# Hand-over between stages: four blocks by token halves, weights four deep, residual adds on VectorE

## Chip, cores and metric

One core of a Trainium2 chip runs the whole kernel. The metric is the device time in microseconds (us) of one execution. Outputs are compared with a float32 reference.

## What is computed

512 tokens and 16 meta tokens of width 1024 pass two layers (differential attention, then a short convolution, each followed by a squared-ReLU MLP of width 4096) and then a third block of pooling and a linear recurrence. All of it hangs on this pattern, four times over:

```python
hres = hres + _rmsnorm(m, norm_g[i, 1])
h = _rmsnorm(hres, norm_g[i, 2])
hres = hres + _rmsnorm(_sqrelu_mlp(h, w_up[i], w_down[i]), norm_g[i, 3])
```

and at the end `x = x + y @ w_out[l]`, `rmsnorm(x, final_gain)`. A stage's output `m` is normed and added to the residual `hres`; its norm is the next stage's input.

## The kernel before

Activations lie transposed: 128 channels on the partitions, KT = 8 rows of channels, and 528, 514 or 512 tokens along the free axis (ALL, NEED, OUT). The token halves part at SPLIT = 272. Each of the 225 weight **blocks** (128 output channels by 1024 inputs) is loaded by SyncE into `raw` (four slots), rounded by ScalarE to `whi` (`split`, L502 and in loops L513), and GpSimd subtracts to get the rest `wlo` (`low`, L442). TensorE makes 8 x 3 products a block (whi x hi, whi x lo, wlo x hi, L1329): in two token pieces where there are over 512 tokens, and in one where there are 512. `whi` and `wlo` have two slots, so the split of block b + 2 waits until block b is done. Blocks alternate between two accumulators in PSUM, `G[0]` and `G[1]` (two banks each); `begin` waits until the block two before was copied out.

Every engine runs its own list in order. Four times a stage ends in an RMS norm and the next starts: index i = 0 (attention output, block b0 = 24 onwards, to the first MLP), 1 (to the convolution input), 2 (convolution output to the second MLP), 3 (to the third block's input projection, blocks 192 to 216, where a chain of feature work for four head pairs runs on ScalarE and VectorE under the blocks). At such a **hand-over**:

- TensorE (`last_blocks`) does blocks 6 and 7 of the old stage by token halves, first halves first, then the second halves with the norm's sum (`post_stat`, L1313 and L1317) for the first half of the tokens between them. `first_blocks` then does the new stage's blocks 0 and 1 by halves; block 0 goes row by row behind VectorE, with a product that sums the next norm's squares (`stat_tile`, L1302) before each row.
- VectorE (`last_tiles`) copies the tiles out (L855, L858), adds their squares (L849), takes the reciprocal of the root (L832), scales a row by gain and rstd into `t1` (L897), and makes the low part of the input (`low_x`, L838).
- GpSimd (`residual`, L450) adds `t1` to `hres`; ScalarE (`prenorm`) rounds the row to `xh` (L537) and squares it (L541).

In an MLP's first product each block is copied out with ReLU and rstd (L934), squared twice on ScalarE, and VectorE makes the low part (L925). After block 216, GpSimd makes the four pooled groups (L475 to L487); TensorE's four products of them stand among the steps of the recurrence.

## Time and profile before

| | us |
|---|---|
| median of 3 runs (lowest, highest) | 1746.52 (1742.81, 1751.23) |
| the profiled execution, its time | 1749.39 |
| its span in the trace | 1747.6 |
| TensorE busy (94% of the span) | 1648.2 |
| VectorE, ScalarE, GpSimd busy | 773.7, 621.3, 623.2 |

The mean granted clock of TensorE is 0.974 of full speed. A matmul counts as busy until its result is out, so in a stretch where each waits for the one before, TensorE reads as busy and yet does less than it can: the number of matmuls in a stretch says more than its busy time.

### The profile page before, as it was taken

What the parts mean: (1) busy time and instruction counts of PE and PEld (TensorE: products, weight loads), DVE (VectorE), ACT (ScalarE), POOL (GpSimd) and SP (SyncE); (2) the same over time, 40 slices, a digit from 0 to 9 for tenths busy, and PEclk for the clock granted to TensorE, in tenths of its full rate; (3) what the DMA queues carried; (4) which work ended last, traced back from release to release, by engine and by line L of the source; (5) the groups of instructions that cost most, each with busy time, mean ns of one, the idle gap of its engine ahead of it and who ended that gap; (6) DMA issues with size and microseconds to landing.
All of it is one profiled execution on the core that took longest, in us unless ns stands there. A gap on an engine that the chain in (4) does not pass through costs nothing.

```text
span 1747.6 us, 31109 instructions
## 1 busy us (share of the span) xinstructions
PE 1648.2 (94%) x12448; PEld 1441.7 (82%) x12448; DVE 773.7 (44%) x1260; ACT 621.3 (36%) x1127; POOL 623.2 (36%) x315
## 2 busy tenths in 40 slices
PE   7999998899999999899998999999998999899895
PEld 6888876889999999799977788888886777777664
DVE  3334442554232221654427441414138995455426
ACT  5556663343222222422224432313135434232312
POOL 2222221444444344444435444444435444500021
PEclk9999998999999999999999999999999999899888
DMA  5112110222332322123221333333321222000001
GB/s 194 51 49 61 50 49 25 73 73 86 97 90 92 97 87 96 61 73 96 86 90 42 97 97 96 96 90 93 95 85 61 73 88 93 15 3 2 2 25 48
DMA packets 35400, 125.64 MB, mean 72 GB/s; under 512 B 3920, under 2 KB 4048, under 8 KB 35280
## 3 DMA queue, kind: packets, MB, share of 16 engines
q1 hardware_dynamic: 35280, 123.90, 22.6%
q8 instruction: 93, 1.52, 0.4%
q14 instruction: 27, 0.22, 0.0%
HBM read 121.79 MB, written 2.10 MB: 71 GB/s over the span
## 4 chain that ended last, share of the span: by engine, by line
PE 80%; DVE 11%; POOL 3%; issue 3%; ACT 2%; DMA 0%; DVEq 0%; SPq 0%; POOLq 0%; ACTq 0%
PE G L1329 63%; PE G L1571 4%; PE PV L1571 3%; PE PV L1444 2%; DVE t L897 2%; PE ST L1571 2%; DVE rstd L832 1%; POOL wlo L442 1%; PE PO L1571 1%; DVE xl L838 1%; PE G L1420 1%; PE ST L1302 1%; POOL t L475 1%; PE PO L1433 1%; DVE t L1088 1%
## 5 line engine op out<-in xcount | busy, mean ns | idle before, releaser
L442 POOL TENSOR_TENSOR wlo<-raw,whi 128x1024 fp32r<-128x1024 f32 x225 | 547.5, 2434 | 1065.2 <-ACT whi L502 704.2
L1329 PE MATMUL G<-xh,whi 128*128 128x256 f32 (+3 forms) x1552 | 387.2, 313 | 4.7 <-POOL wlo L442 2.7
L1329 PE MATMUL G<-xl,whi 128*128 128x256 f32 (+3 forms) x1552 | 368.5, 301 | 0.0
L1329 PE MATMUL G<-xh,wlo 128*128 128x256 f32 (+3 forms) x1552 | 366.7, 300 | 0.0
L1329 PE MATMUL G<-ah,whi 128*128 128x258 f32 (+2 forms) x992 | 269.6, 319 | 10.7 <-POOL wlo L442 6.2
L1329 PEld LDWEIGHTS G<-xh,whi 128*128 128x128 f32 x1552 | 251.3, 189 | 29.9 <-issue 11.3
L513 ACT ACTIVATE whi<-raw 128x1024 fp32r<-128x1024 f32 x112 | 118.8, 1060 | 429.5 <-PE G L1329 429.5
L1329 PE MATMUL G<-al,whi 128*128 128x258 f32 (+2 forms) x992 | 267.2, 317 | 0.0
L1329 PE MATMUL G<-ah,wlo 128*128 128x258 f32 (+2 forms) x992 | 266.9, 316 | 0.0
L1329 PEld LDWEIGHTS G<-xl,whi 128*128 128x128 f32 x1552 | 250.9, 189 | 12.4
L1329 PEld LDWEIGHTS G<-xh,wlo 128*128 128x128 f32 x1552 | 251.8, 189 | 10.2
L502 ACT ACTIVATE whi<-raw 128x1024 fp32r<-128x1024 f32 x113 | 119.5, 1058 | 288.7 <-PE G L1329 254.4
L1329 PEld LDWEIGHTS G<-ah,whi 128*128 128x128 f32 x992 | 169.4, 191 | 25.6 <-POOL wlo L442 7.2
L1329 PEld LDWEIGHTS G<-al,whi 128*128 128x128 f32 x992 | 168.8, 191 | 12.7
L1329 PEld LDWEIGHTS G<-ah,wlo 128*128 128x128 f32 x992 | 168.6, 191 | 12.7
L925 DVE TENSOR_TENSOR al<-act,ah 128x512 f32 (+2 forms) x64 | 115.7, 1807 | 98.3 <-ACT act L582 98.3
L858 DVE TENSOR_TENSOR m<-G,m 128x514 f32 (+5 forms) x52 | 33.9, 651 | 209.3 <-PE G L1329 209.3
L934 DVE SCALAR_TENSOR_TENSOR t<-G,rstd 128x514 f32<-128x514 f32 (+1 forms) x64 | 44.3, 693 | 105.8 <-PE G L1329 105.5
L1329 PE MATMUL G<-x2h,whi 128*128 128x512 f32 (+1 forms) x216 | 87.5, 405 | 0.9 <-POOL wlo L442 0.9
L1302 PE MATMUL ST<-sq,con 128*128 128x256 f32 (+2 forms) x160 | 56.4, 446 | 28.8 <-DVE xl L838 21.6
L1329 PE MATMUL G<-x2l,whi 128*128 128x512 f32 (+1 forms) x216 | 82.0, 380 | 0.0
L1329 PE MATMUL G<-x2h,wlo 128*128 128x512 f32 (+1 forms) x216 | 81.6, 378 | 0.0
(275 smaller groups left out, 2023.8 us busy)
## 6 DMA issues: line engine op xcount, KB each, us to landing
raw<-weights_dram SPq DMA_DIRECT2D x225, 512.0 KB, 3.5
hres<-xT_dram SPq DMA_DIRECT2D x8, 264.0 KB, 6.0
out_dram<-hres SPq DMA_DIRECT2D x8, 256.0 KB, 2.1
con<-consts_dram SPq DMA_DIRECT2D x1, 512.0 KB, 9.2
mat<-mats_dram SPq DMA_DIRECT2D x1, 512.0 KB, 10.0
con<-consts_dram SPq DMA_DIRECT2D x1, 392.0 KB, 5.5
vec<-vecs_dram SPq DMA_DIRECT2D x1, 203.0 KB, 2.6
```

What stands on the lines that cost most here:

```text
L442: nc.gpsimd.tensor_tensor(wlo[:, s % 2], raw[:, s], whi[:, s % 2].bitcast(F32), ALU.subtract)\
L475: nc.gpsimd.tensor_tensor(dst[:, PAD:], src[:, PAD:], src[:, PAD - sh:PAD + SEQ - sh], ALU.add)\
L502: nc.scalar.activation(whi[:, s % 2], raw[:, s], ACT.Copy).then_inc(hi_ready, 1)
L513: nc.scalar.activation(whi[:, s2 % 2], raw[:, s2], ACT.Copy).then_inc(hi_ready, 1)
L858: nc.vector.tensor_tensor(mt, acc_of[:, pos], mt, ALU.add).then_inc(count, 1)
L897: nc.vector.scalar_tensor_tensor(t1[:, k % 2, o], m[:, k, o], gain(*norm, k), rstd[:, s % 2, tokens(cols, half)], ALU.mult, ALU.mult)\
L925: nc.vector.tensor_tensor(tile(al[f % 2], j, slice(0, w)), act2[:, s4 % 2, 0:w], tile(ah[f % 2], j, slice(0, w)).bitcast(F32), ALU.subtract)\
L934: nc.vector.scalar_tensor_tensor(t1[:, s4 % 2, 0:w], G[s4 % 2][:, pos], 0.0, rstd[:, s % 2, c0], ALU.max, ALU.mult).then_inc(tile_out, 1)
L1302: last = nc.tensor.matmul(ST[:, p0:p1], ones, sq[:, k % 2, t0 - cols[0]:t1_ - cols[0]], start=k == 0, stop=k == KT - 1, skip_group_check=True)
L1329: last_of[0] = nc.tensor.matmul(to[:, p0:p1], wt[:, w, ws], xt[:, k, t0 - off:t1_ - off], start=k == 0 and q == 0, stop=k == KT - 1 and q ...
L1444: last = nc.tensor.matmul(PV[0:rows, 0:P], aT[0:nk, t % 2, j, 0:rows], vtok[0:nk, h % 2, j, :], start=j == 0, stop=j == i)
L1571: return nc.tensor.matmul(out_, lhsT, rhs, start=start, stop=stop)
```

## The change

`whi` and `wlo` get four slots and `raw` two. The old stage's blocks 4 to 7 go by token halves (four first halves, then four second halves), and so do the new stage's blocks 0 to 3: blocks 0 and 1 side by side row by row, then blocks 2 and 3. Blocks done by halves have banks of their own (`held`). VectorE takes over the residual add, and the low parts of the new stage's first four weight blocks (`low_w`). The squares for the next norm go into four half-wide slots of `t1`, and TensorE sums them two rows late. In the third block's input projection blocks 4 and 5 move up to steps 2 and 3. In the attention stage the weight split runs three blocks ahead instead of two. Some buffers of the third block now share memory with others.

VectorE's queue at the first hand-over (`m` is the stage's output, `t` is t1, `acc` the sum of squares), before: from the first reciprocal on.

```order
L832 RECIPROCAL rstd<-rms 128x258 [waits rms_ready]
L897 SCALAR_TENSOR_TENSOR t<-m,vec,rstd 128x258 [waits rstd_ready]
L855 COPY m<-G 128x256 [waits block_done]
L897 SCALAR_TENSOR_TENSOR t<-m,vec,rstd 128x258
L849 TENSOR_TENSOR acc<-acc,sq 128x256 [waits psq_added,psq_ready]
L855 COPY m<-G 128x256 [waits block_done]
L897 SCALAR_TENSOR_TENSOR t<-m,vec,rstd 128x258 [waits h_ready]
L838 SCALAR_TENSOR_TENSOR xl<-hres,vec,xh 128x258 [waits x_hi]
```

The same place in the changed kernel, up to the second row:

```order
L869 RECIPROCAL rstd<-rms 128x258 [waits rms_ready]
L893 COPY m<-G 128x256 [waits block_done]
L928 SCALAR_TENSOR_TENSOR m<-m,vec,rstd 128x258 [waits rstd_ready]
L928 SCALAR_TENSOR_TENSOR m<-m,vec,rstd 128x258
L935 TENSOR_TENSOR hres<-hres,m 128x258 [waits t1_ready]
L928 SCALAR_TENSOR_TENSOR m<-m,vec,rstd 128x258
L935 TENSOR_TENSOR hres<-hres,m 128x258 [waits t1_ready]
L876 SCALAR_TENSOR_TENSOR xl<-hres,vec,xh 128x258 [waits x_hi]
L893 COPY m<-G 128x256 [waits block_done]
L887 TENSOR_TENSOR acc<-acc,sq 128x256 [waits psq_added,psq_ready]
L908 TENSOR_TENSOR wlo<-raw,whi 128x1024 [waits hi_ready]
L928 SCALAR_TENSOR_TENSOR m<-m,vec,rstd 128x258
```

The add of a row and the wide subtraction of a weight block (L908) now stand in VectorE's own queue, where a wait for GpSimd (`h_ready`) stood.

TensorE's queue where the new stage begins (`sq` and `t1` hold squares, `acc` their sum), before:

```order
L1313 MATMUL ST<-acc,con 128x256 [waits psq_added,rms_ready]
L1317 MATMUL ST<-sq,con 128x256 [waits psq_ready]
L1302 MATMUL ST<-sq,con 128x258 [waits rms_ready,x_ready,sq_ready,tile_out,lo_ready]
L1329 MATMUL G0<-xh,whi 128x258
L1329 MATMUL G0<-xl,whi 128x258
L1329 MATMUL G0<-xh,wlo 128x258
L1302 MATMUL ST<-sq,con 128x258 [waits sq_ready,x_ready]
```

and in the changed kernel, from the first row of the new stage:

```order
L1416 MATMUL G0<-xh,whi 128x258 [waits tile_out,lo_ready,x_ready]
L1416 MATMUL G0<-xl,whi 128x258
L1416 MATMUL G0<-xh,wlo 128x258
L1416 MATMUL G0<-xh,whi 128x258
L1416 MATMUL G0<-xl,whi 128x258
L1416 MATMUL G0<-xh,wlo 128x258
L1416 MATMUL G0<-xh,whi 128x258 [waits x_ready]
```

A row now carries six matmuls instead of three, the sum of squares stands two rows behind, and the second half's post_stat has moved behind row 4. The diff, cut to its core:

```diff
-POST_SQ, POST_ADD = KT + 2, KT
+HELD = 4
+POST_SQ, POST_ADD = KT + HELD, KT + HELD - 2
+def half_square(j, half):
+    return j + 1 + (HELD if half else 0)
+def half_added(j, half):
+    return j + 1 + (HELD - 1 if half else 0)
+def square_slot(k, half):
+    q = k + KT * half
+    return q % 2, TOK // 2 * (q // 2 % 2)
+def held(cols, j, half):
+    w = cols[1] - cols[0]
+    first = SPLIT - cols[0]
+    if half is None:
+        return [(j, 0, 0, w)] if w <= BANK else [(j, 0, 0, first), ((6, 7, 4, 5)[j], 0, first, w)]
+    if half == 0:
+        return [(j, 0, 0, first)]
+    return [(j, first, first, w)] if w <= BANK else [((6, 7, 4, 5)[j], 0, first, w)]
...
-        raw = sb("raw", [P, 4, D])
-        whi = sb("whi", [P, 2, D], F32R)
-        wlo = sb("wlo", [P, 2, D], F32R)
+        raw = sb("raw", [P, 2, D])
+        whi = sb("whi", [P, 4, D], F32R)
+        wlo = sb("wlo", [P, 4, D], F32R)
...
-            act2 = sb("act2", [P, 2, NW], F32, mlp)
             cb = sb("cb", [P, 3, NW], F32, mlp)
+            act2 = cb[:, 0:2]
...
-                if isinstance(b, int) and b < 4:
+                if isinstance(b, int) and b < 2:
                     return
-                sp.wait_ge(lo_ready, b - 3)
+                sp.wait_ge(lo_ready, b - 1)
                 src = weights[b] if isinstance(b, int) else weights[bass.ds(b, 1)].rearrange("b p n -> p (b n)")
-                sp.dma_start(raw[:, s], src).then_inc(w_loaded[s], 16)
+                sp.dma_start(raw[:, s % 2], src).then_inc(w_loaded[s % 2], 16)
             blocks(sp, 0, NBLK, load)
...
-                if not isinstance(b, int) or b >= 2:
-                    pool.wait_ge(block_done, b - 1)
-                nc.gpsimd.tensor_tensor(wlo[:, s % 2], raw[:, s], whi[:, s % 2].bitcast(F32), ALU.subtract)\
+                if not isinstance(b, int) or b >= 4:
+                    pool.wait_ge(block_done, b - 3)
+                nc.gpsimd.tensor_tensor(wlo[:, s], raw[:, s % 2], whi[:, s].bitcast(F32), ALU.subtract)\
...
-            def residual(i, half, cols):
-                for k in range(KT):
-                    n = 2 * KT * i + KT * half + k + 1
-                    pool.wait_ge(t1_ready, n)
-                    c = tokens(cols, half)
-                    nc.gpsimd.tensor_tensor(hres[:, k, c], hres[:, k, c], t1[:, k % 2, tokens(cols, half, cols[0])], ALU.add)\
-                        .then_inc(h_ready, 1)
             done = 0
-            for i, (b, cols) in enumerate(((B_MLP[0], NEED), (B_CI, NEED), (B_MLP[1], OUT), (B_IN2, OUT))):
-                blocks(pool, done, b + 1 - done, low)
-                residual(i, 0, cols)
-                low(b + 1, 1, (b + 1) % 4)
-                residual(i, 1, cols)
-                done = b + 2
-            blocks(pool, done, B_O2 + 2 - done, low)
+            for b in (B_MLP[0], B_CI, B_MLP[1], B_IN2):
+                blocks(pool, done, b - done, low)
+                done = b + HELD
+            blocks(pool, done, B_O2 + 3 - done, low)
...
-                        split(b + 2, (s + 2) % 4)
+                        split(b + HELD, s)
...
+                def input_row(k, half):
+                    if k < KT:
+                        c = tokens(cols, half)
+                        act.wait_ge(h_ready, 2 * KT * i + KT * half + k + 1)
+                        hi = x2h[:, k, tokens(cols, half, META)] if layer == 2 else xh[:, k, c]
+                        nc.scalar.activation(hi, hres[:, k, c], ACT.Copy, scale=gain(layer, n, k)).then_inc(x_hi, 1)
+                    if k >= 2:
+                        input_square(k - 2, half)
+                def input_square(k, half):
+                    c = tokens(cols, half)
+                    if k + KT * half >= 4:
+                        act.wait_ge(sq_used, sq_base(s) + KT * half + k - 3)
+                    r, o = square_slot(k, half)
+                    nc.scalar.activation(t1[:, r, o:o + c.stop - c.start], hres[:, k, c], ACT.Square).then_inc(sq_ready, 1)
+                for j in range(HELD, KT):
+                    half_square_of(j, 0)
+                stat_root(s - 1, cols, 0)
+                split(new, 0)
+                half_square_of(4, 1)
+                input_row(0, 0)
+                input_row(1, 0)
+                half_square_of(5, 1)
+                split(new + 1, 1)
+                input_row(2, 0)
+                input_row(3, 0)
+                half_square_of(6, 1)
+                split(new + 2, 2)
+                input_row(4, 0)
+                input_row(5, 0)
+                half_square_of(7, 1)
+                split(new + 3, 3)
+                input_row(6, 0)
+                stat_root(s - 1, cols, 1)
+                for k in range(7, KT + 2):
+                    input_row(k, 0)
+                stat_root(s, cols, 0)
+                for k in range(KT + 2):
+                    input_row(k, 1)
+                stat_root(s, cols, 1)
...
-                    split(s + 2, (s + 2) % 4)
+                    split(s + 3, (s + 3) % 4)
...
+            def low_w(b):
+                dve.wait_ge(hi_ready, b + 1)
+                nc.vector.tensor_tensor(wlo[:, b % 4], raw[:, b % 2], whi[:, b % 4].bitcast(F32), ALU.subtract)\
+                    .then_inc(lo_ready, 1)
...
+                def scaled(k, half):
+                    o = tokens(cols, half, cols[0])
+                    nc.vector.scalar_tensor_tensor(m[:, k, o], m[:, k, o], gain(*norm, k), rstd[:, s % 2, tokens(cols, half)],
+                                                   ALU.mult, ALU.mult).then_inc(t1_ready, 1)
+                def residual(k, half):
+                    c = tokens(cols, half)
+                    dve.wait_ge(t1_ready, 2 * KT * i + KT * half + k + 1)
+                    nc.vector.tensor_tensor(hres[:, k, c], hres[:, k, c], m[:, k, tokens(cols, half, cols[0])], ALU.add)\
+                        .then_inc(h_ready, 1)
+                def input_rows(ks, half):
+                    for k in ks:
+                        if k + 1 < KT:
+                            scaled(k + 1, half)
+                        residual(k, half)
+                        if k >= 1:
+                            low_x(i + 1, *pre, k - 1, cols, half)
...
-                half_tile(KT - 2, 0)
-                add_square(i, KT - 3, cols)
-                half_tile(KT - 1, 0)
-                add_square(i, KT - 2, cols, 0)
-                for half in range(2):
-                    stat_recip(s, cols, half)
-                    dve.wait_ge(rstd_ready, stat_count(s, half))
-                    o = tokens(cols, half, cols[0])
-                    for k in range(KT + 2):
-                        if k < KT:
-                            if k >= 2:
-                                dve.wait_ge(h_ready, 2 * KT * i + KT * half + k - 1)
-                            nc.vector.scalar_tensor_tensor(t1[:, k % 2, o], m[:, k, o], gain(*norm, k),
-                                                           rstd[:, s % 2, tokens(cols, half)], ALU.mult, ALU.mult)\
-                                .then_inc(t1_ready, 1)
-                        if k == 5 and half == 1:
-                            stat_recip(s + 1, cols, 0)
-                        if k >= 2:
-                            low_x(i + 1, *pre, k - 2, cols, half)
-                        elif k == 0 and half == 0:
-                            half_tile(KT - 2, 1)
-                        elif k == 1 and half == 0:
-                            add_square(i, KT - 2, cols, 1)
-                            half_tile(KT - 1, 1)
+                for j in range(HELD, KT):
+                    half_tile(j, 0)
+                    add_square(i, j - 1, cols, None if j == HELD else 0)
+                stat_recip(s, cols, 0)
+                half_tile(4, 1)
+                dve.wait_ge(rstd_ready, stat_count(s, 0))
+                scaled(0, 0)
+                input_rows((0, 1), 0)
+                half_tile(5, 1)
+                add_square(i, 4, cols, 1)
+                low_w(new)
+                input_rows((2, 3), 0)
+                half_tile(6, 1)
+                add_square(i, 5, cols, 1)
+                low_w(new + 1)
+                input_rows((4, 5), 0)
+                half_tile(7, 1)
+                add_square(i, 6, cols, 1)
+                low_w(new + 2)
+                input_rows((6, 7), 0)
+                stat_recip(s, cols, 1)
+                low_x(i + 1, *pre, KT - 1, cols, 0)
+                low_w(new + 3)
+                stat_recip(s + 1, cols, 0)
+                dve.wait_ge(rstd_ready, stat_count(s, 1))
+                scaled(0, 1)
+                input_rows(range(KT), 1)
+                low_x(i + 1, *pre, KT - 1, cols, 1)
...
-                post_stat(s - 1, cols, 1)
+                off = META if hi is x2h else 0
+                def rows(j, ks, half):
+                    (g, p0, o0, o1), = held(cols, j, half)
+                    some(bank(g), j, ks, hi, lo, off, [(cols[0] + o0, cols[0] + o1, p0, p0 + o1 - o0)])
+                def start(j):
+                    pe.wait_ge(lo_ready, b0 + j + 1)
+                    pe.wait_ge(tile_out, b0 + j - 3)
                 for half in range(2):
-                    for j in range(2):
+                    if half == 0:
+                        start(0)
+                        start(1)
+                    for k in range(KT):
+                        pe.wait_ge(x_ready, x_base(i + 1) + KT * half + k + 1)
+                        if k >= 2:
+                            stat_tile(s, k - 2, cols, half)
+                        for j in range(2):
+                            rows(j, [k], half)
+                            if half and k == KT - 1:
+                                last_of[0].then_inc(block_done, 1)
+                        if k == 4 and half == 0:
+                            post_stat(s - 1, cols, 1)
+                    stat_tile(s, KT - 2, cols, half)
+                    stat_tile(s, KT - 1, cols, half)
+                    for j in range(2, HELD):
                         if half == 0:
-                            begin(b0 + j)
-                        for k in range(KT):
-                            if j == 0:
-                                pe.wait_ge(x_ready, x_base(i + 1) + KT * half + k + 1)
-                                stat_tile(s, k, cols, half)
-                            some(G[(b0 + j) % 2], (b0 + j) % 2, [k], hi, lo, 0, block_part(cols, half))
+                            start(j)
+                        else:
+                            pe.wait_ge(rms_ready, stat_count(s, j - 2))
+                        rows(j, range(KT), half)
                         if half:
                             last_of[0].then_inc(block_done, 1)
             def last_blocks(i, b0, hi, lo, cols):
-                operands = hi, lo, cols[0]
-                for j in (KT - 2, KT - 1):
-                    begin(b0 + j)
-                    some(G[j % 2], j % 2, range(KT), *operands, part(cols, 0))
+                def rows(j, ks, half):
+                    t = tokens(cols, half)
+                    some(bank(j - HELD), j % 4, ks, hi, lo, cols[0], [(t.start, t.stop, 0, t.stop - t.start)])
+                for j in range(HELD, KT):
+                    pe.wait_ge(lo_ready, b0 + j + 1)
+                    pe.wait_ge(tile_out, b0 + (HELD - 1 if j < HELD + 2 else HELD))
+                    rows(j, range(KT), 0)
                     last_of[0].then_inc(half_done, 1)
-                some(G[0], 0, range(KT // 2), *operands, part(cols, 1))
-                post_stat(2 * i + 1, cols, 0)
-                some(G[0], 0, range(KT // 2, KT), *operands, part(cols, 1))
-                last_of[0].then_inc(block_done, 1)
-                some(G[1], 1, range(KT), *operands, part(cols, 1))
-                last_of[0].then_inc(block_done, 1)
+                for j in range(HELD, KT):
+                    pe.wait_ge(half_out, HELD * i + j - HELD + 1)
+                    if j == HELD:
+                        rows(j, range(3), 1)
+                        post_stat(2 * i + 1, cols, 0)
+                    rows(j, range(3 if j == HELD else 0, KT), 1)
+                    last_of[0].then_inc(block_done, 1)
...
-                elif j >= 2:
-                    product(B_IN2 + j, 1, x_ready, 0, x2h, x2l, OUT, 0)
+                elif j in (2, 3) or j >= 6:
+                    ahead = j + 2 if j < 4 else j
+                    product(B_IN2 + ahead, 1, x_ready, 0, x2h, x2l, OUT, 0)
...
```

## Rows read from the trace of the kernel before

**Rows 1.** The page: busy time of each engine.
```profile
PE 1648.2 (94%) x12448; PEld 1441.7 (82%) x12448; DVE 773.7 (44%) x1260; ACT 621.3 (36%) x1127; POOL 623.2 (36%) x315
```

**Rows 2.** Windows: PE, PEld, DVE, ACT, POOL busy, granted clock, DMA.
```profile
327.00:363.50 36.50, 29.36 (x182) 25.64 (x180) 30.05 (x42) 19.84 (x44) 19.72 (x19) 0.95 0.09 30
1341.20:1484.10 142.90, 140.84 (x584) 107.38 (x584) 117.50 (x116) 62.24 (x73) 60.41 (x23) 1.00 0.28 86
```

**Rows 3.** The chain that ended last: start, us, what.
```profile
294.96 24.80 PE G L1329 x192
320.99 2.39 POOL wlo L442
329.41 1.78 DVE rstd L832
363.45 344.44 PE G L1329 x2880
...
717.53 1.78 DVE rstd L832
...
752.83 126.12 PE G L1329 x1056
...
962.11 334.11 PE G L1329 x1440
```

**Rows 4.** Timeline of DVE, first hand-over.
```profile
326.94 0.42 DVE L849 TENSOR_TENSOR acc<-acc,sq 128x258 f32<-128x258 f32 x1
331.95 2.28 DVE L897 SCALAR_TENSOR_TENSOR t<-m,vec,rstd 128x258 f32<-128x258 f32 x1
...
336.72 0.48 DVE L897 SCALAR_TENSOR_TENSOR t<-m,vec,rstd 128x258 f32<-128x258 f32 x1
337.12 0.47 DVE L838 SCALAR_TENSOR_TENSOR xl<-hres,vec,xh 128x258 fp32r<-128x258 f32 x1
337.51 0.86 DVE L897 SCALAR_TENSOR_TENSOR t<-m,vec,rstd 128x258 f32<-128x258 f32 x1
338.30 0.47 DVE L838 SCALAR_TENSOR_TENSOR xl<-hres,vec,xh 128x258 fp32r<-128x258 f32 x1
...
361.74 0.69 DVE L934 SCALAR_TENSOR_TENSOR t<-G,rstd 128x514 f32<-128x514 f32 x1
363.82 0.69 DVE L925 TENSOR_TENSOR al<-act,ah 128x514 fp32r<-128x514 f32 x1 [1.39 <-ACT act L582]
364.43 0.69 DVE L934 SCALAR_TENSOR_TENSOR t<-G,rstd 128x514 f32<-128x514 f32 x1
```

**Rows 5.** Timeline of POOL: in the first hand-over, and behind block 216.
```profile
331.54 2.39 POOL L442 TENSOR_TENSOR wlo<-raw,whi 128x1024 fp32r<-128x1024 f32 x1 [8.18 <-ACT whi L502]
...
1487.64 1.03 POOL L475 TENSOR_TENSOR t<-zu 128x512 f32<-128x512 f32 x1
```

**Rows 6.** Timeline of PE; idle time before in brackets.
```profile
294.96 0.51 PE L1329 MATMUL G<-ah,whi 128*128 128x258 f32 x2 [2.92 <-POOL wlo L442]
...
326.39 0.28 PE L1329 MATMUL G<-ah,whi 128*128 128x256 f32 x1
...
341.17 0.60 PE L1302 MATMUL ST<-sq,con 128*128 128x258 f32 x2
...
341.97 0.60 PE L1302 MATMUL ST<-sq,con 128*128 128x258 f32 x2
...
1512.32 2.07 PE L1571 MATMUL PV<-Gp,mat 128*128 128x512 f32 x2 [4.28 <-POOL Gp L487]
```

**Rows 7.** Windows behind two long waits, columns as above.
```profile
297.00:299.00 2.00, 2.00 (x11) 2.00 (x11) 0.00 (x0) 0.00 (x0) 0.44 (x1) 0.50 0.80 238
1512.30:1516.00 3.70, 3.68 (x34) 2.17 (x36) 1.18 (x2) 0.00 (x0) 0.00 (x0) 0.50 0.00 0
```

**Rows 8.** The page: weight splits and transfers (median us to landing).
```profile
L502 ACT ACTIVATE whi<-raw 128x1024 fp32r<-128x1024 f32 x113 | 119.5, 1058 | 288.7 <-PE G L1329 254.4
...
raw<-weights_dram SPq DMA_DIRECT2D x225, 512.0 KB, 3.5
```

181 lines of the change are left out of this document (86 added, 95 removed).

## Prediction

> **What bounds the kernel now.** I read the page first: TensorE is busy 94% of the span [rows 1]. Then the chain: two stages run as one piece of TensorE work, 2880 matmuls in 344.4 us and 1056 in 126.1 [rows 3]; that is 0.1195 us for 257 columns, 2.87 us a half block and 5.74 a block, and 344.44 is 60 blocks with nothing to gain. With 512 columns a block takes 24 x 334.11/1440 = 5.57. What is left lies at the seams. In the first hand-over, 327.0 to 363.5, TensorE starts 182 matmuls in 36.5 us [rows 2], where its pace allows 305: some 15 us go although it reads as busy. The chain there runs over VectorE's reciprocals and its rows. VectorE's timeline shows why a row takes 1.18 us: scale, then low part, 0.40 and 0.39 apart when alone, but 0.79 when GpSimd's add runs beside them (337.51 to 338.30), and 2.28 for one beside the subtraction of a weight block that began at 331.54 [rows 4, 5]. TensorE has three products and a sum for each row, 0.80 us (341.17 to 341.97) [rows 6].
>
> **The hand-over before.** I count from the end of block 3 of the old stage to the start of block 4 of the new one. Blocks 4 and 5 take 11.5, first half of 6 2.9, then the wait for block 7's wlo (split after block 5, landing at 320.99 + 2.39, 1.2 us late [rows 3]), first half of 7 2.9: 18.5. There the second halves start, at 326.39 [rows 6]; the reciprocal follows 3.0 later, at 329.41, and the new stage's block 2 at 363.45, that is 37.05 behind 326.39. At the next one I put the second halves 3.0 ahead of 717.53 and get 752.83 - 714.5 = 38.3; the two others give the same 38.3. With blocks 2 and 3 (11.5) the first costs 67.0 and the others 68.3 (67.6 with 512 columns).
>
> **The hand-over after.** No wait for wlo, since four slots let it run ahead: four first halves, 11.5. Call the start of the second halves 0.
> - TensorE: three rows, post_stat at 1.1 to 1.8 (now after three rows and not four), the rest of block 4 to 3.6, blocks 5 to 7 to 12.2.
> - VectorE, with these steps between starts: scale 0.40, low part 0.39, 258-column add or copy 0.35 (0.42 long, 326.94), reciprocal 1.68 [rows 4]. `low_w` is not in the trace: a 514-column subtraction takes 0.69, a 258-column one 0.42, so 1024 columns take about 1.23. The bounds are 1.15 and GpSimd's 2.39. Reciprocal 2.7 to 4.4; rows 0 and 1, then a copy, an add, low_w: first one done 8.9, second 13.0, third 17.1.
> - TensorE waits at block 1's start for the second low_w, 12.2 to 13.05. Rows of six products: 0.80 + 3 x 0.12 = 1.15 (0.72 for the first two, which carry no sum). Row 4 ends 17.95, post_stat 18.65, row 6 20.95. The second reciprocal runs 19.5 to 21.2, the last low part lands 21.6, row 7 ends 22.8, the sums 23.5, the first halves of blocks 2 and 3 29.25.
> - Meanwhile VectorE: low_w, reciprocal of the new norm 24.4 to 26.2, then eight rows of 0.40 + 0.35 + 0.40 = 1.15. It ends at 35.4, and TensorE, which starts these rows at 29.25, is never held: rows end 38.3, second halves of blocks 2 and 3 44.0. Last reciprocal 39.2 to 41.0.
> - Block 4 needs blocks 0 to 2 copied out. In an MLP a block costs VectorE the 2.69 from 361.74 to 364.43, of which it waits 1.39 for the squares [rows 4]: 41.0 + 2 x 2.69 + 0.7 = 47.1, and 0.7 more for one low part held up by GpSimd's 2.39 instruction: third block out at 47.8. In the convolution input there is no such wait: out by 43.1, TensorE goes on at 44.0.
>
> Of the moved work, sixteen adds cost VectorE 5.6 us a hand-over and four low_w 4.6; the sixteen 0.39 us stalls and the 1.8 at 331.95 that go with GpSimd's silence pay 8. GpSimd's queue holds nothing else there. The new transfers for blocks 2 and 3 start only when low_w 0 and 1 free a raw slot, and land 3.5 later [rows 8], at 12.4 and 16.5; ScalarE waits for them in order, but it was busy only 19.8 of 36.5 us [rows 2].
>
> **The sum.**
> - First hand-over: 67.0 - (11.5 + 47.8) = 7.7, less 2.0: a wait of 3.8 us on TensorE is followed by a lower clock. Behind the 2.92 us wait at 294.96 [rows 6] the granted clock reads 0.50, the 1.2 GHz level [rows 7], and 192 matmuls take 24.80 instead of 22.95 [rows 3]: 1.85. Gain 5.7.
> - Second: 68.3 - 55.5 = 12.8, less 0.6 for block 5, which finds VectorE in the convolution: 12.
> - Third: 67.6 - 59.3 - 2.0 = 6.3.
> - Fourth: here the feature chain on VectorE counts too. From 1341.2 to 1484.1 TensorE does 23 blocks of 5.57 (128.1) and the feature products in 142.9, with VectorE busy 117.5 [rows 2]. The upper bound is TensorE alone: 68.3 - 55.5 = 12.8, and some 5 of waits in that stage: 18. The lower bound is VectorE's start on the new blocks: before at 361.74 - 326.39 + 1.25 + 18.5 = 55.1 behind block 3 [rows 4, 6], now at 52.5: 2.6. Between them: before, VectorE's steps 2 to 5 each waited for a block 5.57 apart and then ran late; now blocks 0 to 3 lie ready, and it has caught up when the first pair's sums arrive behind block 5. Walking its queue so, I get the pair's chain 9 us earlier, and take 9.
> - Start of the attention output: its third block waited 2.92 for wlo [rows 6], since two slots were full. Now blocks 2 and 3 are ready; 0.2 remains for the copy-out. 2.7 and the 1.85 of clock: 4.5.
> - Pooling: GpSimd starts it at 1487.64 because the last weight block before it is split behind block 216. Now the last is split behind block 215, 5.57 earlier. TensorE waits 4.28 for the fourth group at 1512.32 [rows 5, 6], and then runs at 0.50 at least to 1516 [rows 7]. The wait goes whole; of the clock I take 3, between the 1.85 found above and half of the stretch if it lasts to about 1522. 7.3.
> - Weights two deep in raw at the start, and one split more ahead of row 6: -0.5.
>
> 5.7 + 12 + 6.3 + 9 + 4.5 + 7.3 - 0.5 = 44.3. The profiled execution took 1749.4, 2.9 above the median; 1749.4 - 44.3 = 1705.1, against the median 1702.
>
> **Two rules of the Trainium skill.** "VectorE: DVE Perf Modes", section on the TRN2 errata, says each SBUF instruction pays a fixed cost, so many small tiles lose against few large ones; this speaks against halves. The trace agrees (0.42 twice against 0.69: 0.15 a split); the sum above has it in its durations, and by the page's (N+151)/0.96 cycles low_w would be 1.22, an estimate that moves nothing. "TensorE: Matmul & The Clock Gate", section on HAM oscillation, says that idle gaps put TensorE back to half rate; the trace agrees (0.50 behind 2.92 idle). Without it the sum would be 44.3 - 4.85 + 4 = 43.5.
>
> **Rivals.**
> - *VectorE becomes the bound of the hand-over* (0.18). It carries every add now. If the steps don't fall to 0.40 (sixteen at 0.79), each hand-over gives back 6.2: 25 us, 1727. For it: the deep mix of semaphores, and VectorE already 30 of 36.5 us busy [rows 2]; against it: 336.72 to 337.12 shows 0.40 with GpSimd quiet.
> - *TensorE nearly dense* (0.14): the copy-out waits vanish behind slack (2 x 5.8) and the fourth hand-over gives 12 instead of 9: 1702 - 15 = 1687.
> - *Slower by the raw ring* (0.04): a raw slot is reused after split 1.06, low 2.39 and transfer 3.5, 7.0 us [rows 5, 8], against two blocks, 11.5. From a transfer of 8.0 us on, every 0.1 costs 0.05 a block, 9 us over some 190 blocks; at 8.5 us it eats the 44, at 8.6 it gives 1711 + 44 = 1755. For it: transfers of the start take longer when many run at once; against it: the median of 3.5 over 225 [rows 8].
> - *The change does nothing that counts* (0.05): what TensorE saves in rows comes back as waits for copy-out and features, at every hand-over: 1742 to 1750.
>
> The forecast itself has 0.59, with its own range 1692 to 1714. The range goes to 1685 and 1728, which takes in the first two rivals. What a measurement can tell is about 0.5%, 9 us. Faster 0.91, same 0.05, slower 0.04.
>
> **What would show it.** Right: four hand-overs of TensorE shortened by about 8, 12, 8 and 9; VectorE rows of 1.15 with no GpSimd instruction beside; no wait for wlo at 295, 321, 709; the fourth pooled group without a wait; a copy-out wait near 3.8 in both MLPs and none in the convolution. Wrong: rows at 1.5 or more; waits of ScalarE for raw in the long stages; the feature chain ending where it did.

## The result, and the profile after

The changed kernel takes 1730.9 us (median of 20 runs, 1715.7 to 1747.0), the kernel before 1746.8 beside it: ratio 0.989, 95% interval 0.9874 to 0.9907. (The ratio is that of the fast runs, which leaves out six of the 20 of the changed kernel.) It is faster, by 16 us where 44 were forecast, and it lies above the range. The profiled execution took 1724.9 us, its span is 1723.0. The forecast's own range was 1692 to 1714, the full one 1685 to 1728.

The page of the changed kernel, busy time of each engine, answers to [rows 1]:
```profile
PE 1644.7 (95%) x12640; PEld 1451.2 (84%) x12640; DVE 792.9 (46%) x1364; ACT 621.7 (36%) x1135; POOL 530.2 (31%) x235
```
Ninety microseconds have gone from GpSimd, twenty came to VectorE. The page does not show where the forecast went wrong. For that I put the two traces side by side at events that both have: the attention output's first 48 matmuls, the first reciprocal of each hand-over (R1 to R4), the first pair's products in the last stage, and the second pair's.

| stretch | before, us | after, us | gain | forecast |
|---|---|---|---|---|
| start of span to attention output | 281.7 | 304.4 | -22.8 | -0.5 |
| attention output to R1 | 47.7 | 38.6 | 9.1 | 4.5 + 7.0 |
| R1 to R2 | 388.1 | 381.0 | 7.1 | 5.7 |
| R2 to R3 | 209.3 | 203.1 | 6.2 | 12 |
| R3 to R4 | 379.1 | 371.0 | 8.1 | 6.3 |
| R4 to the first pair | 179.1 | 182.7 | -3.6 | 9 - 7.0 |
| first pair to second pair (pooling) | 44.5 | 34.6 | 9.9 | 7.3 |
| second pair to the end | 218.2 | 207.6 | 10.5 | 0 |
| sum | 1747.6 | 1723.0 | 24.6 | 44.3 |

(Of a hand-over's gain, 18.5 - 11.5 = 7.0 us lie ahead of its first reciprocal, so the forecast is cut there too.) Three rows are off by more than 3 us to the bad side: attention by 22, the stretch behind R2 by 6, the one behind R4 by 6. The last row is off by 10.5 to the good side.

The hand-over itself came out as forecast. VectorE's timeline in the first hand-over of the changed kernel, answering to [rows 4]; forecast time 0 is 2.7 ahead of the first reciprocal, 340.4:
```profile
343.08 1.76 DVE L869 RECIPROCAL rstd<-rms 128x258 f32<-128x258 f32 x1 [1.80 <-ACT rms L539]
...
346.17 0.48 DVE L928 SCALAR_TENSOR_TENSOR m<-m,vec,rstd 128x258 f32<-128x258 f32 x1
346.57 0.42 DVE L935 TENSOR_TENSOR hres<-hres,m 128x258 f32<-128x258 f32 x1
346.90 0.48 DVE L876 SCALAR_TENSOR_TENSOR xl<-hres,vec,xh 128x258 fp32r<-128x258 f32 x1
...
347.97 1.22 DVE L908 TENSOR_TENSOR wlo<-raw,whi 128x1024 fp32r<-128x1024 f32 x1
```
The steps of a row start 0.40, 0.33 and 0.40 apart, and `low_w` takes 1.22 us (1.23 was estimated). The last reciprocal starts at 379.81, that is at 39.4 (39.2 forecast). In the chain of the changed kernel, answering to [rows 3], block 4 of the MLP starts at 48.1 (47.8 forecast), behind a wait of 3.53 us for the copy-out (3.8 forecast):
```profile
343.08 1.76 DVE rstd L869
...
388.47 334.07 PE G L1416 x2793
```

What the forecast did not have is in the attention stage. First the kernel before, VectorE's timeline about one `kT` block, then GpSimd's at the same time:
```profile
178.20 0.71 DVE L1027 SCALAR_TENSOR_TENSOR kT<-G,rstd 128x528 f32<-128x528 f32 x1 [2.51 <-PE G L1329]
178.83 0.16 DVE L987 RECIPROCAL rden<-den 128x2 f32<-128x2 f32 x1
179.02 0.22 DVE L989 SCALAR_TENSOR_TENSOR coef<-rden,lamd,den 128x1 f32<-128x1 f32 x1
179.28 0.63 DVE L992 SCALAR_TENSOR_TENSOR prob<-prob,coef 128x400 f32<-128x400 f32 x1
```
```profile
179.40 2.75 POOL L442 TENSOR_TENSOR wlo<-raw,whi 128x1024 fp32r<-128x1024 f32 x1 [8.43 <-ACT whi L502]
```
Then the changed kernel, the same two timelines:
```profile
155.26 0.71 DVE L1109 SCALAR_TENSOR_TENSOR kT<-G,rstd 128x528 f32<-128x528 f32 x1 [2.52 <-PE G L1416]
155.88 0.16 DVE L1069 RECIPROCAL rden<-den 128x2 f32<-128x2 f32 x1
156.08 2.07 DVE L1071 SCALAR_TENSOR_TENSOR coef<-rden,lamd,den 128x1 f32<-128x1 f32 x1
158.18 0.64 DVE L1074 SCALAR_TENSOR_TENSOR prob<-prob,coef 128x400 f32<-128x400 f32 x1
```
```profile
155.75 2.38 POOL L466 TENSOR_TENSOR wlo<-raw,whi 128x1024 fp32r<-128x1024 f32 x1 [7.75 <-ACT whi L515]
```
With four slots the split no longer waits for TensorE, so GpSimd's subtraction now starts 0.33 us ahead of the coefficient, a VectorE instruction on one column, and not 0.38 behind it. The coefficient ends with the subtraction (158.15 and 158.13): it is held. By held I mean here that a VectorE instruction takes longer than the same instruction elsewhere and does not end before the GpSimd instruction beside it. Behind it in VectorE's queue stand `prob`, `al` and the next scores. In the window from 155 to 165 TensorE has 48 matmuls at a granted clock of 0.83, where the kernel before has 73 at 1.00 from 178 to 188. The distance from the `kT` to the `vT` copy is 13.69 us in place of 10.43.

The groups of that line from 26 to 290 us, the kernel before and then the changed one, show that it is no single event:
```profile
L989 DVE SCALAR_TENSOR_TENSOR coef<-rden,lamd,den 128x1 f32<-128x1 f32 x32 | 7.0, 220 | 1.1
```
```profile
L1071 DVE SCALAR_TENSOR_TENSOR coef<-rden,lamd,den 128x1 f32<-128x1 f32 x31 | 20.3, 656 | 1.1
```
That is 13.5 us of holding, in eight instructions, seven of them held for 1.8 us or more. The chain's heads (start of the ten value products) are 30.8 us apart before (105.72, 136.54) and 34.0 and 32.5 after:
```profile
110.28 1.50 PE PV L1556 x10
...
144.29 1.50 PE PV L1556 x10
...
178.29 1.50 PE PV L1556 x10
...
210.80 1.50 PE PV L1556 x10
```
The 22.8 us come in parts. Six periods of heads take 184.6 us before (from 62.5) and 201.1 after (from 63.8), 16.5 more, at mean granted clocks of 1.00 and 0.97. The last head then takes 29.8 us at 0.71 against 26.0 at 0.87, and the rest, 2.5 us, lies ahead of the first period and behind the last head. att_pool_wait below is the same program, and there the clock stays at 1.00 over the six periods: 195.0 us, 10.4 more than before. So the holds by themselves cost 1.7 us a head, and up to 3.3 where the clock falls behind them. The last head is another matter: feat_low_vector below, where no coefficient is held, takes 29.8 us at 0.71 for it too.

### The profile page after: what moved, and what is told of

Same layout as the page of the kernel before. It is cut to its first block, busy times and chain, and to the rows that moved or that the text cites. A ratio compares the mean times of both kernels' runs of the same rounds, so it can differ in the third digit from the quotient of the medians.

```text
span 1723.0 us, 31371 instructions
## 1 busy us (share of the span) xinstructions
PE 1644.7 (95%) x12640; PEld 1451.2 (84%) x12640; DVE 792.9 (46%) x1364; ACT 621.7 (36%) x1135; POOL 530.2 (31%) x235
## 4 chain that ended last, share of the span: by engine, by line
PE 84%; DVE 11%; issue 3%; ACT 2%; DMA 0%; DVEq 0%; SPq 0%; ACTq 0%
PE G L1416 64%; PE G L1683 4%; PE PV L1683 3%; PE PV L1556 3%; PE ST L1683 2%; PE ST L1389 2%; PE G L1532 1%; PE PO L1683 1%; DVE rstd L869 1%; PE PO L1545 1%; DVE t L1170 1%; PE ST L1532 1%; DVE acc L1320 1%; DVE wlo L908 1%; DVE xl L876 1%
## 5 line engine op out<-in xcount | busy, mean ns | idle before, releaser
L466 POOL TENSOR_TENSOR wlo<-raw,whi 128x1024 fp32r<-128x1024 f32 x209 | 506.9, 2426 | 1153.1 <-ACT whi L515 715.3
L1416 PE MATMUL G<-xh,whi 128*128 128x258 f32 (+3 forms) x1504 | 374.2, 311 | 13.2 <-DVE t L1014 6.9
L1416 PE MATMUL G<-xl,whi 128*128 128x258 f32 (+3 forms) x1504 | 360.1, 302 | 0.0
L1416 PE MATMUL G<-xh,wlo 128*128 128x258 f32 (+3 forms) x1504 | 358.1, 301 | 0.0
L1416 PE MATMUL G<-ah,whi 128*128 128x256 f32 (+2 forms) x1024 | 281.3, 316 | 4.5 <-DVE al L1145 2.9
L1416 PE MATMUL G<-al,whi 128*128 128x256 f32 (+2 forms) x1024 | 279.4, 314 | 0.0
L1416 PE MATMUL G<-ah,wlo 128*128 128x256 f32 (+2 forms) x1024 | 279.1, 314 | 0.0
L1416 PEld LDWEIGHTS G<-al,whi 128*128 128x128 f32 x1024 | 178.6, 192 | 11.3
L1416 PEld LDWEIGHTS G<-ah,wlo 128*128 128x128 f32 x1024 | 178.4, 192 | 11.5
L1001 DVE TENSOR_TENSOR al<-cb,ah 128x514 f32 (+3 forms) x64 | 117.8, 1841 | 96.3 <-ACT cb L624 96.3
L896 DVE TENSOR_TENSOR m<-G,m 128x514 f32 (+5 forms) x56 | 34.4, 613 | 198.0 <-PE G L1416 198.0
L1014 DVE SCALAR_TENSOR_TENSOR t<-G,rstd 128x512 f32<-128x512 f32 (+2 forms) x64 | 43.2, 675 | 93.7 <-PE G L1416 93.6
L893 DVE COPY m<-G 128x256 f32<-128x256 f32 (+5 forms) x40 | 23.3, 582 | 114.4 <-PE G L1416 114.4
```

The costliest lines, as they stand in the source:

```text
L466: nc.gpsimd.tensor_tensor(wlo[:, s], raw[:, s % 2], whi[:, s].bitcast(F32), ALU.subtract)\
L893: nc.vector.tensor_copy(mt, acc_of[:, pos]).then_inc(count, 1)
L896: nc.vector.tensor_tensor(mt, acc_of[:, pos], mt, ALU.add).then_inc(count, 1)
L1001: nc.vector.tensor_tensor(tile(al[f % 2], j, slice(0, w)), act2[:, s4 % 2, 0:w], tile(ah[f % 2], j, slice(0, w)).bitcast(F32), ALU.subtract)\
L1014: last = nc.vector.scalar_tensor_tensor(t1[:, s4 % 2, o], ps, 0.0, rstd[:, s % 2, cols[0] + o.start:cols[0] + o.stop], ALU.max, ALU.mult)
L1416: last_of[0] = nc.tensor.matmul(to[:, p0:p1], wt[:, w, ws], xt[:, k, t0 - off:t1_ - off], start=k == 0 and q == 0, stop=k == KT - 1 and q ...
```

## The experiments

Clock first, since it sets how times compare. The last stage, from the first pair to the end, takes 242.2 us in the trace of the changed kernel and 260.1 in that of after_again, the same program. Whole times of one kernel scatter by up to 31 us, and so most of what follows is read from the stretch between the attention output and the first pair, the "middle": 1203.3 us before, and 1176.4 to 1177.7 in four traces of the changed kernel's program. Of the kernel before there is one trace. Its medians beside the experiments are 1745.9 to 1749.2 us, so that ratios compare better than times.

**after_again**, the changed kernel unaltered.

> The changed kernel once more, as the base for the three others of this call. Both theories: 1725 to 1735 us, about 0.99 of the kernel before; in its trace the attention heads follow each other every 32.5 or 34.0 us from the second on, against 30.75 in the kernel before, and the attention output's first matmuls start at about 304 us.

1728.1 us (6 runs), ratio 0.986 (0.9826 to 0.9894). The attention output starts at 304.95, heads are 34.0 or 32.5 us apart: the loss repeats. (Its profiled execution was one of the longest, 1744.5 us; its middle is 1177.6 all the same.)

**att_act_wait.** ScalarE's split waits as before:
```diff
                 if s < 24:
+                    act.wait_ge(block_done, s + 1)
                     split(s + 3, (s + 3) % 4)
```


> The changed kernel, with one wait put back: in the attention stage the high split of a weight block waits for the same block of TensorE as before, so both the split on ScalarE and the subtraction on GpSimd come at their old places. Theory A (GpSimd's subtraction holds VectorE's small coefficient operation for 2.07 us in place of 0.22, and the gap that follows lets the TensorE clock fall): head period back to 30.75 us, attention output starts near 282 us, no coefficient operation over 0.3 us, time 1725 to 1735 less 20 to 23: about 1707 us. Theory B (the split's early place in ScalarE's queue delays what stands behind it): the same, about 1707. Theory C (the loss comes from another part of the change: raw two deep, the moved tiles): no gain, 1725 to 1735, attention output at about 304 us.

1715.7 us, ratio 0.984 (0.9798 to 0.9881). No coefficient over 0.222 us, heads 30.7 us apart, attention output at 287.31. Theory C (the loss comes from another part of the change) has fallen; A (GpSimd's subtraction holds VectorE) and B (the early split delays what stands behind it) stand. The median came back by 12 us and the attention output by 17.1, not by 20 to 23: in this trace the last head met the lower clock (0.50 from 270 to 280, against 0.84 in the kernel before).

**att_pool_wait and pool_late** were to move only GpSimd's waits. Both edits stood in a branch that GpSimd's hardware loop does not take, so the programs are the changed kernel's:
```diff
-                    pool.wait_ge(block_done, b - 3)
+                    pool.wait_ge(block_done, b - 2 if isinstance(b, int) and b < B_AO + 3 else b - 3)
```


> The changed kernel, with the wait put back on GpSimd alone: the high split on ScalarE stays early, and the subtraction waits for the block of TensorE as before. Theory A: head period 30.75 us, attention output near 282 us, about 1707 us, as with the wait on ScalarE. Theory B: ScalarE's split is as early as in the changed kernel, so nothing comes back: head period 32.5 to 34 us, 1725 to 1735 us. Theory C: nothing comes back either.

> The changed kernel, where GpSimd's subtractions for the first four blocks of the second output projection (those ahead of the pooling) wait for all but the last block of the projection before, so that the pooling starts after 1484 us (by about 5 to 8 us later than in the changed kernel), as in the kernel before. My theory (the pooling's last result is on the path, 7.3 us in the prediction, 9.9 by the two traces): 6 to 10 us slower than the changed kernel, 1732 to 1743 us. Rival (the pooling is covered by the chain of the first pair, and the 10 us come from elsewhere): within 2 us of the changed kernel.

1724.5 us (6 runs) and 1726.2 us (12 runs): two more repeats, and nothing on either theory. They do show how far the start of the attention output scatters in this one program: 304.4, 305.0, 297.1 and 302.1 us in its four traces.

**sub_after_prob** separates A from B. The split stays early, and GpSimd's subtraction alone is tied to VectorE's last difference of the turn:
```diff
             done = 0
+            for b in range(B_AO + 3):
+                if b >= 3:
+                    pool.wait_ge(a_done, max(tiles(b - 3), default=-1) + 1)
+                low(b, b, b % 4)
+            done = B_AO + 3
```


> The changed kernel, with the high split on ScalarE left early in the attention stage (as changed), and GpSimd's subtraction tied to VectorE's last difference of the same turn, so that it can't lie over the coefficient operation (these 27 subtractions are issued one by one and not in a loop, so that the wait is really theirs; the wait of att_pool_wait stood in the branch that the loop doesn't take and changed nothing). Theory A (GpSimd's subtraction holds VectorE's coefficient operation): no coefficient operation over 0.3 us, heads 30.7 us apart, attention output near 287 us, time as att_act_wait, 12 to 20 us below the changed kernel: 1706 to 1716 us. Theory B (the early split in ScalarE's queue delays what stands behind it): heads stay 32.5 to 34 us apart, 1725 to 1731 us.

1711.7 us, ratio 0.9803 (0.9761 to 0.9844). GpSimd's timeline shows the new releaser, and VectorE's the coefficient beside it:
```profile
179.52 2.36 POOL L466 TENSOR_TENSOR wlo<-raw,whi 128x1024 fp32r<-128x1024 f32 x1 [8.85 <-DVE prob L1078]
```
```profile
178.55 0.22 DVE L1075 SCALAR_TENSOR_TENSOR coef<-rden,lamd,den 128x1 f32<-128x1 f32 x1
178.81 0.64 DVE L1078 SCALAR_TENSOR_TENSOR prob<-prob,coef 128x400 f32<-128x400 f32 x1
```
Heads 30.7 us apart, attention output at 281.14 (281.69 in the kernel before). B has fallen: the split's early place costs nothing that can be seen, and the subtraction's place is the cause. How much it costs, one pair of traces can't say. In the eleven traces without a held coefficient (this one, att_act_wait and all that are built on either) the attention output starts at 281.1 to 288.1 us, 284.8 on average, against 297.1 to 305.0, 302.2 on average, in the four with it: 17 us, 9 at least.

**coef_one_input** asks what is held. In the changed kernel, the coefficient takes one tensor and two per-partition scalars:
```diff
-                nc.vector.scalar_tensor_tensor(coef[0:rows, t:t + 1], rden[0:rows, 1, t:t + 1], lamd[0:rows, 4:5],
-                                               den[0:rows, 0, t:t + 1], ALU.mult, ALU.mult)
+                nc.vector.tensor_scalar(coef[0:rows, t:t + 1], rden[0:rows, 1, t:t + 1], lamd[0:rows, 4:5],
+                                        den[0:rows, 0, t:t + 1], ALU.mult, ALU.mult)
```


> The changed kernel, where the coefficient operation takes one tensor and two per-partition scalars in place of two tensors and one scalar (the same product). If GpSimd's subtraction holds a VectorE operation only where that reads two tensors from SBUF: no coefficient operation over 0.3 us, and the hold moves to the next operation, the difference of 128x400, which also reads two: 2.0 to 2.5 us in place of 0.64; head period 32.5 to 34 us and 1715 to 1747 us as the changed kernel. If it is something of this operation's line or of its tiny operands: neither is held, head period 30.7 us, 12 to 20 us below the changed kernel. If any VectorE operation is held: the coefficient operation at about 2 us as before.

1727.5 us (2 runs). VectorE's timeline, then GpSimd's:
```profile
152.01 0.27 DVE L1071 TENSOR_SCALAR coef<-rden,lamd,den 128x1 f32<-128x1 f32 x1
152.32 2.19 DVE L1074 SCALAR_TENSOR_TENSOR prob<-prob,coef 128x400 f32<-128x400 f32 x1
```
```profile
151.69 2.39 POOL L466 TENSOR_TENSOR wlo<-raw,whi 128x1024 fp32r<-128x1024 f32 x1 [7.68 <-ACT whi L515]
```
The coefficient passes under the subtraction, and the next instruction with two SBUF tensors is held in its place, 2.19 us for 0.64. The heads come 32.3 us apart and the attention output starts at 292.9, with the clock at 1.00 over the six periods. An instruction that reads one operand from PSUM is not held: in the kernel before, `al` lies under a subtraction (179.40 to 182.15, above) in six turns and takes no longer than elsewhere:
```profile
179.93 0.76 DVE L998 SCALAR_TENSOR_TENSOR al<-ST,gsub,ah 128x514 fp32r<-128x514 f32 x1
```
This is what the Trainium skill says in "SBUF — State Buffer", section "Who interferes with whom": an instruction of VectorE with two SBUF inputs contends with a GpSimd one that reads SBUF, whoever issues first keeps the shared ports for its whole instruction, and the other stands still. The traces agree in both orders: 2.07 us for 0.22 where GpSimd was first, and 2.75 for 2.38 on GpSimd where `prob` was.

**low_on_gpsimd** undoes one part, on top of att_act_wait: GpSimd takes the four low parts of each hand-over again.
```diff
-                done = b + HELD
+                done = b
...
             def low_w(b):
-                dve.wait_ge(hi_ready, b + 1)
-                nc.vector.tensor_tensor(wlo[:, b % 4], raw[:, b % 2], whi[:, b % 4].bitcast(F32), ALU.subtract)\
-                    .then_inc(lo_ready, 1)
+                return
```


> att_act_wait, with the low parts of the four blocks of each hand-over (4 x 1.22 us on VectorE) given back to GpSimd, the residual rows left on VectorE. If GpSimd's subtraction holds VectorE's operations that read two operands from SBUF, as the coefficient operation in the attention stage suggests, VectorE saves 4.9 us of work at each of four hand-overs and waits up to 4 x 2.38 us for it: 0 to 4.6 us slower at each, 1708 to 1734 us, and residual rows or new low parts of x of 1.5 to 2.7 us stand in the trace. If there is no such hold, 3 to 5 us faster at each: 1690 to 1700 us.

1734.2 us, ratio 0.9924 (0.9898 to 0.995), the top of the expectation; the middle takes 1197.6 us against att_act_wait's 1177.4. At each hand-over TensorE gets to block 4 some 4.2 us later. VectorE's rows over 2 us stand there:
```profile
330.41 2.58 DVE L877 SCALAR_TENSOR_TENSOR xl<-hres,vec,xh 128x258 fp32r<-128x258 f32 x1
...
335.46 2.59 DVE L877 SCALAR_TENSOR_TENSOR xl<-hres,vec,xh 128x258 fp32r<-128x258 f32 x1
```
VectorE's 1.22 us are a cheaper way to do it than GpSimd's 2.38.

**residual_on_gpsimd** undoes another part, on top of att_act_wait: the residual rows go back.
```diff
+                for half in (0, 1):
+                    for k in range(KT):
+                        c = tokens(cols, half)
+                        pool.wait_ge(t1_ready, 2 * KT * i + KT * half + k + 1)
+                        nc.gpsimd.tensor_tensor(hres[:, k, c], hres[:, k, c], m[:, k, tokens(cols, half, cols[0])], ALU.add)
```


> att_act_wait, with the residual rows of the hand-overs back on GpSimd (0.64 to 0.82 us each), VectorE keeping the four low parts of the weights. The step of the prediction (a row costs VectorE 1.15 us, residual included, and VectorE's queue sets the next stage's input): without the residual the row costs 0.48 us for the scaling and about 0.5 for the low part of x, but each row now goes through a third engine, so 1.18 us per row as in the kernel before: no change in a row's pace, within 3 us at each hand-over, 1708 to 1722 us. Rival (VectorE is the bound, and relieving it gives 16 x 0.4 us back at each): 6 us faster at each, about 1690 us.

1722.3 us (7 runs, 1706.9 to 1725.5). The middle takes 1180.1 us, 2.7 more than att_act_wait: within 3 us as expected over all four, and the rival (6 us faster at each) has fallen. Where the residual runs hardly matters: beside GpSimd's adds VectorE's scaling takes 0.86 to 0.97 us in place of 0.48, and that eats what it saves.

**pool_late2** puts the pooling back to its old place, on top of att_act_wait.
```diff
-            blocks(pool, done, B_O2 + 3 - done, low)
+            blocks(pool, done, B_O2 + 4 - done, low)
...
-            blocks(pool, B_O2 + 3, KT - 3, low)
+            blocks(pool, B_O2 + 4, KT - 4, low)
```


> att_act_wait, with GpSimd's subtraction for one more block of the second output projection ahead of the pooling: its split waits for the last block of the projection before, so the pooling starts some 4 us after the last feature block, where it stood in the kernel before (+3.95 us; -1.4 us in the changed kernel). (The edit of pool_late stood in a branch that the loop doesn't take and changed nothing; that run is a repeat of the changed kernel.) My theory: TensorE's wait for the last pooled result, 4.28 us before and none after, comes back with about 4 us, and the lower clock behind it costs 3 to 5 us more: 5 to 10 us over att_act_wait, 1713 to 1725 us. Rival (the wait is covered by the chain of the first pair): within 2 us of att_act_wait.

1715.9 us, the same as att_act_wait in the medians, where 5 to 10 more were expected; 14 to 23 us of scatter in either kernel can hide that. TensorE's timeline shows the wait back to the hundredth:
```profile
1492.19 1.86 PE L1684 MATMUL PV<-Gp,mat 128*128 128x512 f32 x2 [4.28 <-POOL Gp L500]
```
From first to second pair it takes 40.2 us against 34.6: 5.6 us of the 9.9 that the change gained there. The other 4.3 go with the clock behind the wait. In the kernel before it reads 0.50 from 1512.3 to 1520 and 0.70 from there to 1529; in pool_late2 it reads 0.54 from 1492.2 to 1495.9 and 1.00 from there on. By these windows an estimate of the clock's share is 6.5 us against 1.7.

**held_whole** takes the token halves from blocks 2 and 3 of a new stage, on top of sub_after_prob, whose repeat **sub_after_prob2** ran beside it.
```diff
-                        if half == 0:
+                        if half:
                             start(j)
-                        else:
+                            rows(j, range(KT), 0)
                             pe.wait_ge(rms_ready, stat_count(s, j - 2))
-                        rows(j, range(KT), half)
-                        if half:
+                            rows(j, range(KT), 1)
```


> sub_after_prob, where blocks 2 and 3 of a new stage are no longer computed by token halves (first half between VectorE's two halves of the input rows) but whole, behind the second half's rows. By the timeline of the prediction: TensorE stands at the second half's rows until VectorE has them (rows end at 38.3 as before), then 11.5 us for both blocks instead of 5.75: 49.8 in place of 44.0 for the convolution and the feature stage (+5.8 each), and 49.8 in place of 47.8 in the two MLPs (+2.0 each), and up to 4 us of lower clock behind the longer gap (3 to 6 us at each): first pair's chain 15 to 25 us later (1471 to 1481 us), time 1717 to 1740 us. Rival (the first halves of blocks 2 and 3 cover nothing, since VectorE's rows end late anyway): at most 4 us in all.

> sub_after_prob once more, as the base of this call: 1702 to 1718 us; first pair's chain starts at 1456 us, and from there to the end 242 to 260 us, by how long the clock stays at the lower level in the last stage (which is what differs between two runs of one kernel so far: 242.2 and 260.1 us of the changed kernel).

1716.6 us (5 runs), and the base 1722.4 (6 runs): again the last stage's clock, 243.9 and 260.2 us in the traces, hides what was done. Both times are misses by a little: 1716.6 at the lower edge of 1717 to 1740, and the base above its 1702 to 1718. The middle takes 1187.6 us against 1174.1 and 1174.7, 13 us more (15 to 25 expected). From each first reciprocal to block 4 it takes 48.2, 49.2, 49.0 and 47.7 us, against 45.4, 41.7, 45.1 and 44.2 in sub_after_prob: 2.8, 7.5, 3.9 and 3.5 more, where 2.0, 5.8, 2.0 and 5.8 were expected. The base repeats these times to 0.1 us. So the halves do cover something at every hand-over, and the rival (at most 4 us in all) has fallen.

**two_slots** tightens the squares' wait to that of two slots, on top of sub_after_prob.
```diff
-                    if k + KT * half >= 4:
-                        act.wait_ge(sq_used, sq_base(s) + KT * half + k - 3)
+                    if k + KT * half >= 2:
+                        act.wait_ge(sq_used, sq_base(s) + KT * half + k - 1)
```


> sub_after_prob, where a square of the next norm waits as if it had two slots and not four. By the prediction's rows (1.15 us a row; ScalarE does the high part and the square of a row in about 1.1 us and runs two rows behind): TensorE's sum of row k-2 comes early enough, nothing is held: first pair's chain within 1 us of 1456, time within 3 us of sub_after_prob2. Rival (two slots would hold ScalarE behind TensorE, which takes the two first blocks and the sum for each row): 1 to 2 us for each half, 8 to 16 us in all, 1712 to 1730 us.

1715.5 us, 6.9 under sub_after_prob2 where 3 were allowed. The four reciprocals of the first hand-over lie 16.92, 4.95 and 14.87 us apart against 16.91, 4.95 and 14.86: nothing is held there. The first pair starts at 1465.0, outside the one microsecond that I gave; 2.3 us of that come before the attention output and the rest between R2 and R3 (204.4 against 198.0), where the clock scatters, as the next experiment shows. Four slots bring nothing that can be seen.

**conv_low_vector, feat_low_vector, both_low_vector** take up the two stretches still unexplained. In the changed kernel's trace VectorE's first convolution row, and under it GpSimd, read:
```profile
764.70 2.48 DVE L1133 TENSOR_TENSOR cb<-cb 128x514 f32<-128x514 f32 x1
...
769.31 2.83 DVE L1142 TENSOR_TENSOR m<-m,cb 128x512 f32<-128x512 f32 x1
```
```profile
761.86 4.76 POOL L466 TENSOR_TENSOR wlo<-raw,whi 128x1024 fp32r<-128x1024 f32 x2 [48.22 <-ACT whi L515]
769.21 2.38 POOL L466 TENSOR_TENSOR wlo<-raw,whi 128x1024 fp32r<-128x1024 f32 x1 [2.59 <-ACT whi L515]
```
Both products take 0.69 us in the kernel before. That row has a hold there too, but one: its tensor-scalar takes 2.50 us where the changed kernel's takes 0.49. So the row is stretched by 2.0 us before and by 3.9 after.
```profile
760.32 2.50 DVE L1054 TENSOR_SCALAR m<-cb,vec 128x512 f32<-128x512 f32 x1
```
TensorE pays with a wait (its timeline):
```profile
774.32 0.50 PE L1416 MATMUL G<-xh,whi 128*128 128x258 f32 x2 [2.68 <-DVE cb L1127]
```
And in the feature stage VectorE is busy 72.3 of the 77.6 us from 1338 to 1415.6, and an instruction of it is held for each subtraction; three of twelve, 21.5 us of holding:
```profile
1338.81 2.74 DVE L1173 SCALAR_TENSOR_TENSOR z<-t,vec,z 128x512 f32<-128x512 f32 x1
...
1354.02 2.78 DVE L1198 SCALAR_TENSOR_TENSOR k<-sg,z 128x512 f32<-128x512 f32 x1
...
1369.59 2.83 DVE L1217 SCALAR_TENSOR_TENSOR z<-cs,Gp 128x512 f32<-128x512 f32 x1
```
These holds are not new. The kernel before has them at the same rate, eleven with 20.9 us from 1341 to 1416; two of them:
```profile
1341.75 2.78 DVE L1091 SCALAR_TENSOR_TENSOR z<-t,vec,z 128x512 f32<-128x512 f32 x1
1348.41 2.81 DVE L1091 SCALAR_TENSOR_TENSOR z<-t,vec,z 128x512 f32<-128x512 f32 x1
```
The edits on top of sub_after_prob (waits that keep the count of low parts in order, and GpSimd's skips, are left out here):
```diff
 # conv_low_vector, in the first convolution row
+                if j == 0:
+                    low_w(B_CI + 5)
                 taps = [vec[:, V_CONV + CW * j + i:V_CONV + CW * j + i + 1] for i in range(CW)]
...
+                if j == 0:
+                    low_w(B_CI + 6)
                 dve.wait_ge(a_hi, 40 + j + 1)
 # feat_low_vector, in the feature stage's loop over j
+                if j >= 1:
+                    low_w(b + 3)
                 dve.wait_ge(block_done, b + 1)
```


> sub_after_prob, where VectorE itself takes the low parts of the convolution's sixth and seventh weight block, 1.22 us each, between its own steps, in place of GpSimd. Theory (GpSimd's 2.38 us subtractions hold two products of the first convolution row, 0.69 us each, for 2.5 and 2.8 us, which makes TensorE wait 2.7 us for the fourth block's copy and lowers its clock): both products 0.69 us, the row shorter by 3.9 - 2.4 = 1.5 us plus what the wait for ScalarE hides, the wait of TensorE 0 to 1 us, and from the second to the third hand-over 2 to 4 us less than in sub_after_prob. Rival (the row is late by its place in the queue and not by the hold): the wait stays at 2.7 us or grows by 1.2.

> sub_after_prob, where VectorE itself takes all 24 low parts of the feature stage (1.22 us each) and GpSimd none. In the changed kernel twelve GpSimd subtractions hold VectorE for 21.4 us in all from 1338 to 1415, where VectorE has no idle time but 4.3 us. Theory (VectorE bounds this stage, and the holds are why the fourth hand-over gave 3.4 us and not 9): twelve times 1.22 is 14.6, so about 7 us less up to the end of the second pair's features, and 4 to 8 us less from the fourth first reciprocal to the first pair's chain. Rival (TensorE's blocks bound the stage): VectorE's 29 us of added work are hidden or show, 0 to +10 us.

> Both edits at once: the sum of the two, 6 to 12 us under sub_after_prob in the start of the first pair's chain (1456 to 1465 us there): 1446 to 1458 us; time 1695 to 1712 us, by the clock in the last stage.

| kernel | median, us | ratio (95%) | R2 to R3 | R4 to first pair | middle |
|---|---|---|---|---|---|
| sub_after_prob | 1711.7 | 0.9803 (0.9761 to 0.9844) | 201.1 | 183.9 | 1174.7 |
| sub_after_prob2 | 1722.4 | 0.9851 (0.9814 to 0.9888) | 198.0 | 184.0 | 1174.1 |
| conv_low_vector | 1713.4 | 0.9795 (0.9772 to 0.9818) | 197.9 | 184.0 | 1174.2 |
| feat_low_vector | 1708.0 | 0.9748 (0.9716 to 0.9780) | 203.1 | 176.5 | 1170.2 |
| both_low_vector | 1695.6 | 0.9718 (0.9683 to 0.9753) | 198.0 | 174.9 | 1164.3 |

In the feature stage the theory holds: 7.4 and 9.0 us come back, although VectorE does 29 us more work. In the part that bounds, 12 x 1.22 = 14.6 replaces 21.5 of holds. In the other traces of the changed kernel and its variants the stretch takes 181.1 to 184.5 us, and more in held_whole and low_on_gpsimd (185.6 and 188.2). In the convolution both products are back at 0.69 us and the wait shrinks:
```profile
755.82 0.50 PE L1429 MATMUL G<-xh,whi 128*128 128x258 f32 x2 [0.30 <-DVE cb L1135]
```
In sub_after_prob and its repeat the wait is 1.9 us, since the second hold falls on `al` (2.02 us) and not on a product. The stretch takes 197.9 and 198.0 us with the edit, and 198.0 to 204.4 in the kernels without it that keep the hand-over as it is; the one at 198.0 is sub_after_prob2, with its wait of 1.9. So the edit takes away the wait. In the 30 us that begin 50 us behind R2 the granted clock reads 1.00 in all three traces at 198, and 0.94 and 0.95 in the changed kernel (203.1) and in sub_after_prob (201.1). Whether 3 to 5 us come back thus hangs on whether the clock falls behind the wait, and conv_low_vector against sub_after_prob2 shows no gain at all (197.9 and 198.0). both_low_vector, expected at 1695 to 1712 us with the first pair at 1446 to 1458, comes in at 1695.6 and 1445.4. It is 51 to 54 us faster than the kernel before by its medians, and 2.8% by its ratio, the fastest kernel run here.

## Why the prediction was wrong

**The step that failed** is one of the cover, that is, of what lies beside what: moving the split one block ahead was costed at -0.5 us for the kernel's start alone, and attention, with everything else that is not a hand-over, at nothing. I had the hold in front of me ([rows 4], 331.95, 2.28 us beside a subtraction) and asked only where GpSimd fell silent, never where its remaining 209 subtractions would move to. In the attention stage they moved by 0.7 us against VectorE's coefficient and held it for 13.5 us. The stage came out 22.8 us longer in the profiled pair, and sub_after_prob's trace has all of it back. Over all traces the cure is worth 17 us on average. The last head's share of the 22.8, 3.8 us, goes with a clock that kernels without the hold meet too. That is the largest of three steps that failed; the two others are under the second and the fourth hand-over.

**The hand-over's timeline** was right within 0.4 us at every point of the first hand-over: `low_w` landing at 8.8, 12.9, 17.0 (8.9, 13.0, 17.1), TensorE held until 13.1 with 0.58 us of wait (13.05), reciprocals at 19.6, 24.6, 39.4 (19.5, 24.4, 39.2), block 4 at 48.1 (47.8). In the convolution input block 4 starts at 44.4 (44.0), in the second MLP at 47.8 (47.8). held_whole shows that the halves of blocks 2 and 3 shorten every hand-over; residual_on_gpsimd and two_slots show that the residual's place and the four slots for the squares hardly matter.

**First and third hand-over**, 7.1 and 8.1 against 5.7 and 6.3: right, 1 to 2 us too low. I had taken 2.0 off each for the clock behind the copy-out. In the profiled execution the clock did not fall there: it reads 1.00 behind both waits. In att_act_wait it does fall (0.66 in the first 3.6 us behind the first wait, 0.88 in the next 4), and these stretches take 382.5 and 372.5 us against 381.0 and 371.0: gains of 5.6 and 6.6. So the term was right in kind and 0.5 too large, and this time it wasn't due.

**Second**, 6.2 against 12: TensorE got to block 4 at the time forecast, but I charged only 0.6 for block 5, which finds VectorE in the convolution. It waits 2.7, for a row that two holds stretch by 3.9, and the clock falls behind the wait (0.94). Without those two holds the stretch gains 11.3 and 11.4. In the other kernels that keep the hand-over it gains 4.9 to 8.2, and 11.3 once, in sub_after_prob2, where the wait is 1.9 and the clock stays at 1.00. So the wait is shown, and that it costs 6 us only together with the clock.

**Fourth**, 9 - 7.0 = 2 against -3.6: of the two bounds, 2.6 and 18 for the whole, the trace sits at 7.0 - 3.6 = 3.4, at the lower. The step that I took between them, VectorE catching up on blocks that lie ready, needs VectorE to have room. It had little, before or after: 33.9 us of holds lie in the kernel before's 117.5 busy us of [rows 2], which I had read as plain work, and 34.6 us in the changed kernel from 1338 to the first pair. With VectorE doing the low parts itself the stretch takes 176.5 and 174.9, gains of 2.6 and 4.2, so 9.6 and 11.2 in all. That the first comes near the 9 is luck, since that edit was no part of the forecast.

**Start of the attention output**, 9.1 against 11.5: the wait for the low part is gone as forecast; in att_act_wait this stretch takes 36.2, a gain of 11.5. What lacked in the changed kernel is clock: 38.6 us at 0.91 on average, against 36.2 at 0.99. The attention stage's late heads are not the reason, since sub_after_prob2, which has none, takes 38.7 at 0.91. What decides between the two was not found.

**Pooling**, 9.9 against 7.3: the wait of 4.28 went whole, by pool_late2 worth 5.6 with its clock. I took 3 for the clock, and the change gained 5.6 beyond the wait.

**The end**, 10.5 us in the profiled pair that no step foresaw, goes with the clock of the last stage. Four traces of the changed program take 207.6 to 225.5 us there, against 218.2 in the one trace before, so the gain belongs to the run. That is the likely reason why the medians differ by 16 us and the traces by 25.

**The rivals.** The one on VectorE named the right engine and the wrong place: it priced sixteen steps at 0.79 in each hand-over, where steps take 0.40, and 1727 us was near the outcome by accident. TensorE was not nearly dense: it waits 3.53 and 3.39 us for the copy-out in the two MLPs. That the change does nothing has fallen with the four hand-overs. Nothing showed of the raw ring.

**Two sums of the prediction** are off, and neither decides anything. Four `low_w` at the 1.23 us of its own estimate are 4.9 us and not 4.6. The third hand-over sets 59.3, which is worked out for 514 columns, against 67.6 for 512; with 11.1 us for its two old blocks it would gain 0.4 more.

## What to carry to other kernels

When a change lets an engine run further ahead, list what its instructions will lie beside at their new time, and not only what they stop colliding with. A hold that is already there is easily read as work: look for instructions that take longer than their like. Here, a GpSimd subtraction did no harm once a semaphore of VectorE's own queue placed it behind VectorE's last instruction with two SBUF inputs; and where VectorE was the bound, it was cheaper to do the work there (1.22 us) than to be held by it (up to 2.2). And where the clock scatters the whole time by 1%, compare stretches between events that both traces have, and more than one trace of each kernel.

## What had not been expected of the hardware

A VectorE instruction on one column waits as long as one on 512: 2.07 us for 0.22, to the end of GpSimd's 2.38. A scan and a one-input tensor-scalar on 512 columns were held too (3.43 for 1.22 us at 1383.78, 2.64 for 0.42 at 1391.16 in the changed kernel), while the one-column tensor-scalar of coef_one_input was not (0.27).

The last stage has the same instructions in sub_after_prob and in the changed kernel, and takes 260.0 us in one trace and 242.2 in the other; after_again, the changed kernel unaltered, takes 260.1. The second and third 45 us behind the first pair, granted clock in the column behind POOL; the changed kernel first, then sub_after_prob:
```profile
1525.80:1570.80 45.00, 41.26 (x827) 34.20 (x827) 25.53 (x72) 12.83 (x23) 0.00 (x0) 0.96 0.01 3
1570.80:1615.80 45.00, 41.47 (x841) 34.50 (x839) 25.94 (x73) 11.05 (x21) 0.00 (x0) 0.96 0.01 2
```
```profile
1500.90:1545.90 45.00, 42.37 (x716) 34.95 (x716) 21.95 (x57) 11.46 (x20) 0.00 (x0) 0.81 0.01 2
1545.90:1590.90 45.00, 41.82 (x698) 34.33 (x694) 22.58 (x59) 10.13 (x20) 0.00 (x0) 0.81 0.01 2
```
TensorE is as busy in both, at 0.96 and at 0.81. What decides which of the two a run gets was not found.
